# First output-projection step of a one-core decoder layer: the squares and the turned state stand in two groups around a half product

## What is computed

```python
merged = concat([rms_norm(att) * g_out_att, rms_norm(y_conv) * g_out_conv])   # 512 + 512 columns
h = h + merged @ w_out                                                        # the output projection
h = h + hier_moe(rms_norm(h))                # 32 experts, two of them for each token
h = h + (p @ w_ple_proj) * sigmoid(rms_norm(h) @ w_ple_gate)
```

## Time and profile before

| | us |
|---|---|
| median of three runs | 1107.14 |
| lowest and highest run | 1103.04, 1111.93 |
| span of the profiled execution | 1109.7 |
| PE busy in it | 1062.5 (96%) |
| DVE busy in it | 478.6 (43%) |
| ACT busy in it | 287.8 (26%) |
| mean granted PE clock, share of full speed | 0.979 |

### The profile page before, as it was taken

One profiled execution on the slowest core, in us unless ns is written; L12 is line 12 of the kernel. 1 busy time (PEld: TensorE's weight loads), 2 busy tenths in 40 slices (PEclk: granted clock), 3 DMA queues, 4 the chain that ended last, 5 costly groups with the idle time before them and its releaser, 6 DMA issues.

```text
span 1109.7 us, 15103 instructions
## 1 busy us (share of the span) xinstructions
PE 1062.5 (96%) x5738; PEld 604.8 (55%) x5738; DVE 478.6 (43%) x1109; ACT 287.8 (26%) x597; POOL 155.5 (14%) x171
## 2 busy tenths in 40 slices
PE   6999999999999999999999999889999997989997
PEld 5888875666666666655555555324443332335443
DVE  4836635787412323232546566161111111046675
ACT  2332323777211211101111113111111111135431
POOL 0000001035301010000111111231322211030000
PEclk9999999899899999999999999989999999989999
DMA  9613214930734244346575217899999999884421
GB/s 320 162 39 114 72 49 142 275 66 2 266 132 125 104 153 136 136 157 237 231 300 183 89 71 261 324 388 375 417 416 406 419 420 404 349 303 166 141 76 76
DMA packets 90905, 235.78 MB, mean 212 GB/s; under 512 B 21046, under 2 KB 48606, under 8 KB 76176
## 3 DMA queue, kind: packets, MB, share of 16 engines
q1 hardware_dynamic: 80192, 205.80, 51.0%
q0 software_dynamic: 9920, 26.38, 6.3%
q10 hardware_dynamic: 720, 2.62, 0.6%
HBM read 203.83 MB, written 35.65 MB: 216 GB/s over the span
## 4 chain that ended last, share of the span: by engine, by line
PE 87%; DMA 5%; DVE 4%; ACT 1%; issue 1%; POOL 1%; SPq 0%; POOLq 0%; DVEq 0%; ACTq 0%
PE pair L2699 15%; PE pair L2400 13%; PE pair L2912 13%; PE pair L2763 10%; PE pair L3016 7%; PE pair L2934 5%; PE pair L3011 3%; PE pair L2534 2%; DMA R<-in_w_up 2%; PE pair L2508 2%; PE pair L2549 2%; PE pair L2899 1%; PE pair L2611 1%; PE pair L2628 1%; DMA R<-in_w_in 1%
## 5 line engine op out<-in xcount | busy, mean ns | idle before, releaser
L2699 PE MATMUL pair<-R 128*128 128x352 f32 x576 | 183.7, 468 | 0.0
L2912 PE MATMUL pair<-R 128*32 128x512 f32 (+2 forms) x896 | 154.4, 613 | 5.4 <-DMA R<-in_w_up 3.2
L2400 PE MATMUL pair<-R 128*128 128x256 f32 x672 | 150.7, 384 | 2.6 <-DVE R L1597 2.6
L2400 PEld LDWEIGHTS pair<-R 128*128 128x128 f32 x672 | 128.0, 193 | 21.2 <-DVE R L1597 3.2
L2699 PEld LDWEIGHTS pair<-R 128*128 128x128 f32 x576 | 107.0, 193 | 55.8 <-issue 6.8
L2763 PE MATMUL pair<-R 128*128 128x512 f32 x256 | 118.4, 614 | 0.0
L2912 PEld LDWEIGHTS pair<-R 128*32 128x32 f32 (+2 forms) x896 | 49.2, 127 | 95.1 <-issue 90.5
L2133 DVE TENSOR_TENSOR R<-pair,R 128x256 f32<-128x256 f32 x21 | 8.9, 425 | 210.7 <-ACT R L1410 210.7
L2934 PE MATMUL pair<-R,bias 128*32 128x512 f32 (+2 forms) x448 | 76.3, 596 | 3.1 <-issue 2.5
L2763 PEld LDWEIGHTS pair<-R 128*128 128x128 f32 x256 | 48.2, 195 | 54.3 <-issue 53.7
L3016 PE MATMUL pair<-R 128*128 128x512 f32 x168 | 73.0, 593 | 0.0
(11 more groups left out here) (351 smaller groups left out, 1372.5 us busy)
## 6 DMA issues: line engine op xcount, KB each, us to landing
R<-in_w_gate SPq DMA_DIRECT2D x32, 1024.0 KB, 12.6
R<-in_w_up SPq DMA_DIRECT2D x32, 1024.0 KB, 16.1
R<-in_w_down SPq DMA_DIRECT2D x32, 1024.0 KB, 17.3
R<-in_x_prompt SPq DMA_DIRECT2D x16, 512.0 KB, 4.0
R<-in_cache_k SPq DMA_DIRECT2D x8, 1024.0 KB, 5.1
R<-in_cache_v SPq DMA_DIRECT2D x8, 1024.0 KB, 4.9
R<-y_dram SPq DMA_DIRECT2D x16, 512.0 KB, 5.3
R<-in_w_in SPq DMA_DIRECT2D x4, 1536.0 KB, 12.9
```

The lines of the kernel that those rows point to most:

```text
L2400: last = mm(qbank(p, part, k), lhs[:, c, :], rhs[:, c, :], start=(c == 0), stop=(c == 3))
L2699: last = mm(bk[b][:, 0:n], wB[q % 2][:, c, which, :], xT[:, c, lo:lo + n], start=(c == 0), stop=(c == DC - 1))
L2912: last = mm(bk[2 + u][r, :].rearrange("p (w f) -> p w f", w=2), xgT[u][:, c, r], wgu[s][:, :, c, :], start=(c == 0), stop=(c == DC - 1))
```

## The change

`conv_squares` and `out_conv` get arguments. At `i` = 0 PE does the squares of tiles 0 to 5, then column half 0 of `out_conv(0)`, then the squares of tiles 6, 7 and of the sample tile, the sample squares and the turned state, then column half 1. The three waits that stood ahead of `out_conv(0)` (`y_scaled`, `y_done`, `masked`) now stand ahead of half 0. No instruction is added or removed; the semaphores rise at the same instructions as before.

```diff
-        def conv_squares():
-            pe.wait_ge(S("y_sum"), CC)
-            pe.wait_ge(S("ss_scored"), 2)
-            for t in range(TILES):
+        def conv_squares(first, end):
+            if first == 0:
+                pe.wait_ge(S("y_sum"), CC)
+                pe.wait_ge(S("ss_scored"), 2)
+            for t in range(first, end):
                 n = P if t < PT else SAMP
                 last = mm(bk[7][0:n, t:t + 1], y_sum[:, P * t:P * t + n], ones[:, 0:1], start=True, stop=True)
-            last.then_inc(S("ssc_full"), 1)
+            if end == TILES:
+                last.then_inc(S("ssc_full"), 1)
...
-        def out_part(i, lhs, c0, pair, done, full):
+        def out_part(i, lhs, c0, pair, done, full, sides=(0, 1)):
...
-            for j in range(2):
+            for j in sides:
...
             out_att(i)
             if i == 0:
-                conv_squares()
-                sample_squares()
-                conv_state()
+                conv_squares(0, 6)
                 pe.wait_ge(S("y_scaled"), CC)
                 pe.wait_ge(S("y_done"), 3 * CC)
                 pe.wait_ge(S("masked"), NB)
+                out_conv(0, (0,))
+                conv_squares(6, TILES)
+                sample_squares()
+                conv_state()
+                out_conv(0, (1,))
+                continue
```

More of the change, by code:

```diff
@@ L2770, in out_att, with out_conv @@
             out_part(i, aT, 0, 0, "hA_done", "oA_full")
-        def out_conv(i):
-            out_part(i, yT, CC, 1, "h_done", "oC_full")
+        def out_conv(i, sides=(0, 1)):
+            out_part(i, yT, CC, 1, "h_done", "oC_full", sides)
         def router(i):
```

## The result

The changed kernel takes 1113.45 us (median of 20 runs), the kernel before 1109.75 us (median of 20). The ratio is 1.0041, with a 95% interval of 1.0027 to 1.0054: slower by 3.7 us in the medians and by 3 to 6 us by the interval. (The ratio is not the quotient of the two medians, which is 1.0033.) One run of the changed kernel took 4450.29 us and is left out of the ratio; without it the median is 1113.42. The loss is less than 1%, while single runs of the kernel before lie up to 9.3 us apart (1103.04 to 1112.30), so only many runs of each can tell it from no change. The forecast was 3.7 us over a median of 1107.14 that three runs had given; with twenty runs that median is 2.6 us higher, and so is the time measured.

What follows compares the result with a forecast made beforehand. PE was taken to bound the kernel (87% of the last chain). Starting 2.0 us late after waiting for tile 2, plus 1.7 for a new clock fall, gave 3.7 over 1107.1: 1110.8 us, cases 1106.2 to 1111.9, range 1104 to 1116.

Steps and rivals of the forecast that it cites:

- through tile 2: Main case: tile 2's reload comes late and PE waits for it; chance 0.38 with a new clock fall, 0.22 without.
- The clock: At out_conv(0) on PE: splitting the narrow work avoids the half clock; 1.72 us won, bounds nothing and 1.72.
- The turned state, 3.47 us later: Behind half 0 on PE: its start moves from 533.35 to 536.82, and DVE's first residual moves with it.
- 0.95 us left at the router: Router's transposes on PE: waits for late DVE leave 0.95 of the 1.72 us won; start at 543.77.
- Transfers 3.47 us later: SP's first load, weights, tile 0's store and tile 2's reload all move 3.47 us; bounds no later and 3.47.
- PE waits 2.9 us: Ahead of out_att(3): PE waits 2.9 us for tile 2's residual and starts 2.0 us later than before.
- the first rival: Tile 0's store not held behind the weights, tile 2 under 0.55 us late: 0.95 us won, 1106.2; chance 0.12.
- 3.7 us at the rank with a new fall: Tile 1's rank on PE: 2.0 us late plus 1.7 for a new clock fall, which covers the choice's 0.45.
- Step 7: Behind the wait at out_att(3): a new clock fall is likelier than not, taken as 1.72 us, bounds 0 and 1.72.
- the fall of before is not in every execution: Rival: without its fall, before ends about 1.0 us sooner, so the change costs 3.5 or 4.7 us; chance 0.12.
- lost in the experts: Rival: the expert weight stream, from about 708 to 940 us, absorbs the delay, giving 1107.1; chance 0.10.
- carried to the end whole: From tile 1's rank to the end: no PE slack up to the experts, so all 3.7 us stay.

Runs made afterwards that it cites:

- early_split: Kernel before with the squares in two groups around half 1 of the attention product, turned state not late: 0.9984, later 0.9982 (1108.15 us).
- before_spread: Kernel before with SP issuing store and reload of each of the first four tiles ahead of one expert's weights: 1110.50 us, ratio 1.0009.
- before_late: Kernel before with one more SP wait, until both halves of the first convolution product are done, ahead of its first load: 1114.19 us, ratio 1.0045.
- after_spread: Changed kernel with SP issuing store and reload of each of the first four tiles ahead of one expert's weights: ratio 0.9981, once more 1.0004.

## Why the prediction was right, step by step

The forecast was slower by 3.7 us, through tile 2, with a new fall of the clock; slower by 3.7 us it was in the medians, through tile 2 and with that fall. By its steps, on the ruler from the first square (531.17 before, 527.26 after):

1. *The clock.* Taken as 1.72 us won at the place; the two halves run at full clock, and no trace with two groups has a fall. Right, though the forecast said itself that the trace had no row of this pattern; it was a guess that came true.
2. *The turned state, 3.47 us later.* Measured 5.61 behind the first square (532.87 - 527.26) against 2.18: 3.43.
3. *0.95 us left at the router.* Measured 12.56 against 13.55: 0.99. The two waits, 0.33 and 0.65 us, are those that were worked out.
4. *Transfers 3.47 us later.* SP's first load stands 3.43 us later (9.73 against 6.30), the reload of tile 2 only 2.91 us later (31.61 against 28.70). From the first load to the reload it took 21.88 instead of 22.40 us. That half microsecond is scatter between executions: in the second trace of the change it took 22.37 us, and the reload came 3.41 us later than in before (32.11 against 28.70). That the store's landing hardly depends on its issue is borne out by early_split, where it was issued 1.70 us earlier than in before on the ruler from `out_att(0)` and the reload followed only 0.44 us earlier. The Trainium skill ("DMA: Bandwidth & Descriptors", section on queues, rings and completion order) says that completion on an issuing engine need not follow the order of issue. For the small store behind large loads it did follow it in both kernels: the store landed 1.3 us after the last weights, and took 16.5 and 17.9 us behind them against 2.6 us ahead of them.
5. *PE waits 2.9 us.* Measured 2.29 in one trace, with the reload that came half a microsecond sooner, and 2.74 in the other; the first rival's condition, less than 0.55 us of lateness, was far off.
6. and 7. *3.7 us at the rank with a new fall.* The product behind the wait takes 1.70 us more, the rank starts 3.06 us later on this ruler (45.69 against 42.63), and 3.53 in the second trace. The 0.6 us less than forecast in the first is mostly that of step 4. That the clock fell is right, but the reading behind it does not hold. Step 7 took 3.5 us without wide products for more than the 2.35 us after which the clock had not fallen; but those 2.35 us are idle time alone. Counted as the 3.5 us are, from wide product to wide product, that stretch of before lasts 4.48 us (696.25 to 700.73), and the product behind it runs at full speed:

```profile
689.22 7.03 PE L2834 MATMUL pair<-R 128*128 128x512 f32 x16
698.59 1.13 PE L2899 MATMUL pair<-ident,R 128*128 128x128 f32 x8 [2.35 <-DMA R<-m_dram,lists]
700.73 7.07 PE L2912 MATMUL pair<-R 128*32 128x512 f32 x64 [1.00 <-DVE R L2128]
```

Counted as idle time, the change's fall came after 2.29 us, which is less than 2.35. So these rows could not tell whether the clock would fall; that it did was partly luck.

The rival that the fall of before is not in every execution is half shown: both traces of before have it, and one of the three other traces with an undivided run has not. Its price of 1.0 us was too low where early_split tries it: with PE 1.7 us earlier and the turned state in its old place, nothing was held by tile 2, and the rank came 1.69 us sooner. The rival "lost in the experts" is not borne out: the loss is in the medians.

Two things stay open. In both traces of before the clock also fell in the last tile's product, near 660 us, which took 8.81 us there and 7.11 in both traces of the change; that gave the change 1.7 us back (from the rank to the last logits 99.03 us before, 97.32 after). This fall does not come with the order of before on PE: before_spread and before_late have that order, and the product takes 7.11 us in them as in all the other traces. Why only the two traces of before have it was not tried. And the loss was not carried to the end whole, as the forecast had it. On the ruler from `out_att(0)` the change is 1.4 us behind at the last logits (149.96 against 148.60), after this fall, and 3.5 at the end of the span (588.99 against 585.47; 2.7 in the second pair of traces). So 2.2 of the 3.5 us in the first pair are made behind 670 us, where falls of the clock lie at other times in every execution, and no run shows what makes them. That late transfers cause the loss rests on the medians of after_spread and before_late, not on this pair of spans.

## What to carry to other kernels

When work is moved back on an engine that is never idle, follow each semaphore that it raises to the last transfer behind it: here 1.7 us won on the busiest engine were paid back with more, 25 us later, since a wait on SP stood ahead of 6 MB and a store that PE needed stood behind them. A small transfer on which an engine depends belongs ahead of bulk loads that are not needed for a hundred microseconds. The same split, put where nothing hangs on the moved part, kept its gain up to tile 1's rank; in the medians it was worth 1.7 and 2.2 us, at the edge of what these runs can tell from nothing.

## What the hardware showed that was not expected

- The clock falls though PE is busy without a gap: 2.6 us of products with one moving column and of narrow transposes were followed by 3.4 us at 1.2 GHz in four of five traces. Two such runs of 1.3 us each, with 3.5 us of wide products between them, were followed by none in eight.
- The fall does not come every time for the same order on PE (8.73 us in before, 7.03 us in before_spread for the same product), nor for the same program (from 288 to 296 us the granted clock was 1.00 in one trace of the change and 0.60 in the other), so one trace is not the median.
- Behind a wait of 3.37 us the clock was once at half for over 6 us (before_late, 569 to 575.3 us), and the product lost 3 us (10.12 against 7.13) instead of 1.7.
